# Two layers and an expert block on one core: shared first modulation, rows turned by transposes, modulation pieces moved, constants multiplied in waits

## The reference

```python
for layer in range(2):
    shift_m, scale_m, gate_m, shift_f, scale_f, gate_f = split(silu(c) @ ada_w[layer] + ada_b[layer], 6)
    h = rmsnorm(x, pre_m) * (1 + scale_m) + shift_m
    x = x + gate_m * rmsnorm(mixer[layer](h), post_m)
    h = rmsnorm(x, pre_f) * (1 + scale_f) + shift_f
    x = x + gate_f * rmsnorm((silu(h @ w_gate) * (h @ w_up)) @ w_down, post_f)
# mixer 0: state space model and latent attention; mixer 1: gated linear attention
# (chunks of 64) and sparse attention of three branches (compressed, selected, window)
h = rmsnorm(x); x = x + merged(moba(h), gmlp(h)) @ w_out         # second block
h = rmsnorm(x); m = rmsnorm(mem); x = x + cross_attention(h, m)
h = rmsnorm(x); x = x + peer_ffn(h)                              # 16384 experts, dense here
return rmsnorm(x)
```

## Time and profile before

| | |
|---|---|
| median of 3 runs | 2046.96 us (2045.36 to 2047.48) |
| profiled execution, its own time | 2044.72 us |
| its span | 2042.9 us |
| mean granted TensorE clock | 0.978 of full |
| PE busy | 1922.0 us (94%) |
| DVE busy | 1378.7 us (67%) |
| ACT busy | 986.7 us (48%) |
| POOL busy | 263.4 us (13%) |

### The profile page before, as it was taken

One profiled execution on the slowest core, in us unless ns is written; L12 is line 12 of the kernel. 1 busy time (PEld: TensorE's weight loads), 2 busy tenths in 40 slices (PEclk: granted clock), 3 DMA queues, 4 the chain that ended last, 5 costly groups with the idle time before them and its releaser, 6 DMA issues.

```text
span 2042.9 us, 33499 instructions
## 1 busy us (share of the span) xinstructions
PE 1922.0 (94%) x13340; PEld 1773.0 (87%) x13340; DVE 1378.7 (67%) x2511; ACT 986.7 (48%) x1432; POOL 263.4 (13%) x121
## 2 busy tenths in 40 slices
PE   5899899988998789999998999999999999999998
PEld 5887799988967589998997889999998888999997
DVE  4898765647956664335756548988878887666665
ACT  5445544454435354445554545566653334444444
POOL 1001044430001024441000047100000000000000
PEclk8999999999999799999999999999999999999999
DMA  7663466645654245555444344477776866555452
GB/s 300 228 203 127 157 250 247 234 179 199 205 181 169 73 166 195 186 186 181 165 145 142 127 145 166 166 209 220 219 220 227 300 255 227 187 225 196 176 204 106
DMA packets 94234, 392.82 MB, mean 192 GB/s; under 512 B 7648, under 2 KB 41584, under 8 KB 55552
## 3 DMA queue, kind: packets, MB, share of 16 engines
q1 hardware_dynamic: 94080, 390.69, 55.0%
HBM read 372.83 MB, written 15.73 MB: 190 GB/s over the span
## 4 chain that ended last, share of the span: by engine, by line
PE 75%; DVE 14%; ACT 3%; issue 2%; DMA 0%; POOL 0%; DVEq 0%; ACTq 0%
PE ps L563 10%; PE ps L565 10%; PE ps L564 10%; PE acc L559 9%; PE acc L560 9%; PE acc L561 9%; DVE wlo L1281 3%; PE acc L563 3%; PE acc L565 3%; PE acc L564 3%; DVE arena L1310 2%; PE ps L1236 1%; PE acc L1236 1%; PE ps L626 1%; PE ps L1009 1%
## 5 line engine op out<-in xcount | busy, mean ns | idle before, releaser
L2300 ACT ACTIVATE whi<-raw 128x1024 fp32r<-128x1024 f32 x559 | 589.5, 1059 | 494.3 <-PE acc L561 274.1
L1281 DVE TENSOR_TENSOR wlo<-raw,whi 128x1024 fp32r<-128x1024 f32 x460 | 567.9, 1242 | 312.3 <-ACT whi L2300 311.4
L563 PE MATMUL ps<-hhi,whi 128*128 128x256 f32 x1824 | 521.2, 286 | 9.5 <-ACT hhi L2412 5.4
L564 PE MATMUL ps<-hlo,whi 128*128 128x256 f32 x1824 | 516.6, 283 | 0.0
L565 PE MATMUL ps<-hhi,wlo 128*128 128x256 f32 x1824 | 516.6, 283 | 0.0
L563 PEld LDWEIGHTS ps<-hhi,whi 128*128 128x128 f32 x1824 | 350.2, 192 | 14.6 <-ACT hhi L2412 6.1
L564 PEld LDWEIGHTS ps<-hlo,whi 128*128 128x128 f32 x1824 | 350.3, 192 | 2.9
L565 PEld LDWEIGHTS ps<-hhi,wlo 128*128 128x128 f32 x1824 | 350.1, 192 | 0.0
L1281 POOL TENSOR_TENSOR wlo<-raw,whi 128x1024 fp32r<-128x1024 f32 x99 | 245.2, 2480 | 683.1 <-ACT whi L2300 682.8
L559 PE MATMUL acc<-whi,chi 128*128 128x512 f32 x752 | 295.6, 393 | 3.5 <-DVE wlo L1281 1.9
L560 PE MATMUL acc<-whi,clo 128*128 128x512 f32 x752 | 294.0, 391 | 0.0
(11 more groups left out here) (443 smaller groups left out, 2418.6 us busy)
## 6 DMA issues: line engine op xcount, KB each, us to landing
raw<-in_peer_down SPq DMA_DIRECT2D x64, 1024.0 KB, 5.0
raw<-in_peer_up SPq DMA_DIRECT2D x64, 1024.0 KB, 5.1
arena<-in_ada SPq DMA_DIRECT2D x80, 512.0 KB, 4.8
raw<-in_w_gate SPq DMA_DIRECT2D x22, 1024.0 KB, 4.8
raw<-in_w_up SPq DMA_DIRECT2D x22, 1024.0 KB, 5.2
raw<-in_w_down SPq DMA_DIRECT2D x22, 1024.0 KB, 4.8
arena<-spill SPq DMA_DIRECT2D x14, 1024.0 KB, 7.0
spill<-hT_t SPq DMA_DIRECT2D x22, 448.0 KB, 6.4
```

Source lines behind the costliest of these rows:

```text
L563: e.matmul(out, hi, xh, start=start, stop=False, skip_group_check=True)
L564: e.matmul(out, hi, xl, start=False, stop=False, skip_group_check=True)
L1281: e.tensor_tensor(out=lo, in0=w, in1=hi.bitcast(F32), op=ALU.subtract).then_inc(*X(("lo", j)))
L2300: e.activation(hi, w, ACT.Copy, scale=1.0).then_inc(*self.A(("hi", j)))
```

## The change

1. **First modulation shared.** In every one of the four groups DVE now makes k = 0, 1, 4, 5 and ACT scales k = 2, 3, 6, 7 (`BY_PE`); PE sums ACT's four tiles and DVE's one. DVE adds each group's bias inside the loop of the next one. The slab of `w_low` is loaded before the last 1 MB of the modulation, the first ring piece after the second slab, and the first blocks of `w_low` are cut by DVE instead of POOL.
2. **Rows turned.** `ve_unit` writes x times the root ([128 x 512], two for each half of the tokens) instead of a diagonal, and `pe_norm` turns it with transposes. `pe_rows` uses transposes too.
3. **Order at the junctions.** The block after the first is rounded inside the junction (`se_junction`, `se_norm`), the one after it behind the norm; DVE cuts it after its first pair of tiles.
4. **Modulation's pieces.** The six pieces that hung on `w_nks`, `w_nvs` and `w_out1a` and the one forced before the gate's rows stand in linear attention now, as 2, 3 and 2. In the sparse attention DVE normalises the linear attention's output before it cuts `w_out1a`, cuts a block while ACT exponentiates, and `pct` is turned after the first branch.
5. **Constants in the waits.** Where a junction precedes ffn0, mix1, ffn1, mix2 and the expert layer, PE multiplies a matrix of ones by the constants 16 times before the first half's transposes, 4 times before the second's and 10 times before the first linear layer (`KEEP`).

```diff
+KEEP = (16, 4, 10)
-FIRST = (("w_low", 0, 0), ("w_low", 0, 1), ("w_low", 1, 0), ("w_glr", 0, 0), ("w_mqk", 0, 0))
+FIRST = (("w_glr", 0, 0), ("w_mqk", 0, 0))
+BY_PE = (2, 3, 6, 7)
...
+    def pe_keep(self, e, ps, n):
+        for _ in range(n):
+            e.matmul(ps, self.m.ones, self.m.kc_t[:, 0:128], start=True, stop=True, skip_group_check=True)
...
-    def pe_norm(self, e, nm, x):
+    def pe_norm(self, e, nm, keep=KEEP):
...
         for tt in range(2):
-            e.wait_ge(*self.at("diag", nm, tt))
+            self.pe_keep(e, self.banks.tile(nm, "turned", 3)[:, 128:256], keep[tt])
             for j in range(8):
+                if j % 4 == 0:
+                    e.wait_ge(*self.at("unit", nm, tt, j // 4))
                 o = (j % 2) * 256 + tt * 128
-                i = e.matmul(self.banks.tile(nm, "turned", j // 2)[:, o:o + 128], x[:, tt, j * 128:(j + 1) * 128],
-                             m.diag[:, tt, :], start=True, stop=True, skip_group_check=True)
+                i = e.transpose(self.banks.tile(nm, "turned", j // 2)[:, o:o + 128], m.upd[:, tt, j * 128:(j + 1) * 128],
+                                m.ident)
...
-    def ve_diag(self, e, nm, tt):
+    def ve_unit(self, e, nm, tt, x):
...
+        for half in range(2):
+            sl = slice(512 * half, 512 * half + 512)
+            e.tensor_scalar(out=m.upd[:, tt, sl], in0=x[:, tt, sl], scalar1=m.small[:, 50 + tt:51 + tt], scalar2=None,
+                            op0=ALU.mult).then_inc(*self.V(("unit", nm, tt, half)))
...
         t.then_inc(*self.P(("full", "w_ngate"), ("whole", "w_ngate", 0), ("gated", "P")))
+        self.pe_pieces(e, 2)
...
         self.pe_cmp_hidden(e, 1)
+        self.pe_pieces(e, 3)
         self.pe_cmp_turn(e, 1)
         e.wait_ge(*self.at("out", "gla_state", 2, 2))
         for h in range(4):
+            if h == 3:
+                self.pe_pieces(e, 2)
...
     def se_junction(self, e, post, norm, first):
...
         self.se_acc_square(e, post, 1, 0)
+        self.cut_hi(e, self.W.last(first, 0) + 1)
         self.se_x_square(e, norm, post, 0, 0)
...
         for g in range(4):
             for h in range(2):
+                if (g, h) == (3, 1):
+                    e.dma_start(self.W.slab(0)[0], D["w_low"][0]).then_inc(self.W.slots[0], 16)
```

More of the change, by code:

```diff
@@ L693, in pe_ada, with pe_pieces @@
             i.then_inc(*self.P(("full", "ada", layer, g)))
+    def pe_pieces(self, e, n):
+        for _ in range(n):
+            self.pe_ada(e)
     def pe_ada_until(self, e, layer, part):
@@ L1384, in ve_normed @@
         whole(1)
+        if first:
+            self.cut_lo(e, V, self.W.last(first, 0) + 1)
         low(0)
@@ L1453, in ve_sum @@
         self.ve_eps(e, norm, 0, 48)
-        self.ve_diag(e, norm, 0)
+        self.ve_unit(e, norm, 0, self.m.x)
         self.ve_add_x(e, post, 1, 1)
@@ L1510, in ve_pro @@
             self.ve_eps(e, "mix0", tt, 48)
-            self.ve_diag(e, "mix0", tt)
+            self.ve_unit(e, "mix0", tt, m.x)
         e.wait_ge(self.landed["pos"], 16)
@@ L1874, in ve_nsa @@
                     *V(*([("hvx",)] if ht and j == 3 else [])))
-        self.ve_linear(e, "w_nks", 0, 8, 2)
-        self.ve_linear_tok(e, "w_nvs", 0, 8)
-        e.wait_ge(*self.at("full", "vb"))
-        e.tensor_tensor(out=m.vb, in0=bc(self.banks.tile("vb")[:, 0:64].unsqueeze(1), [128, 8, 64]),
-                        in1=bc(m.kc("ind").unsqueeze(2), [128, 8, 64]), op=ALU.mult).then_inc(*V(("out", "vb")))
+        self.ve_linear(e, "w_nks", 0, 8, 2, ada=False)
         e.wait_ge(*self.at("rstd", "gla"))
@@ L1888, in ve_nsa @@
                 *V(("normed", "gla", j)))
+        self.ve_linear_tok(e, "w_nvs", 0, 8, ada=False)
+        e.wait_ge(*self.at("full", "vb"))
+        e.tensor_tensor(out=m.vb, in0=bc(self.banks.tile("vb")[:, 0:64].unsqueeze(1), [128, 8, 64]),
+                        in1=bc(m.kc("ind").unsqueeze(2), [128, 8, 64]), op=ALU.mult).then_inc(*V(("out", "vb")))
         for eng in "PA":
@@ L1925, in ve_nsa @@
                 self.ve_scores(e, f"nsa{qt}{br}", 8, nk, 0.125, lambda hs, n: m.ab[:, qt, hs, 0:nk], m.St1,
-                               gate=m.ng[:, qt, 8 + 8 * br:16 + 8 * br])
-                self.ve_out(e, "w_out1a", range(at, at + 2))
+                               gate=m.ng[:, qt, 8 + 8 * br:16 + 8 * br],
+                               ahead=self.W.last("w_out1a", 2 * at + 1, 512) + 2)
+                self.ve_out_by_rows(e, "w_out1a", range(at, at + 2), ada=False)
                 self.ve_turn(e, f"nsa{qt}{br}", 8, nk, m.PT1[br])
-            e.wait_ge(*self.at("full", "pct", qt))
-            e.tensor_copy(m.pct, self.banks.tile("pct", qt)[:, 0:128]).then_inc(*V(("out", "pct", qt)))
+                if br == 0:
+                    e.wait_ge(*self.at("full", "pct", qt))
+                    e.tensor_copy(m.pct, self.banks.tile("pct", qt)[:, 0:128]).then_inc(*V(("out", "pct", qt)))
             self.ve_bank_split(e, f"nsa{qt}", m.hH, m.hL, qt)
@@ L2378, in se_junction, with se_norm @@
         self.se_root(e, norm, 1, 48)
-    def se_norm(self, e, nm, src, at=48, ahead=None):
+    def se_norm(self, e, nm, src, at=48, ahead=None, first=None):
         for tt in range(2):
             for half in range(2):
+                if tt and half and first:
+                    self.cut_hi(e, self.W.last(first, 0) + 1)
                 self.se_x_square(e, nm, src, tt, half, at)
@@ L2398, in se_normed @@
         m, A = self.m, self.A
-        if first:
-            self.cut_hi(e, self.W.last(first, 0) + 2)
         for jj in range(4):
@@ L2599, in se_ffn @@
         self.cut_hi(e, self.W.last(f"w_down{layer}", 16 * 11 - 1) + 1)
-        self.se_junction(e, f"ffn{layer}_post", ("mix1", "mix2")[layer])
+        self.se_junction(e, f"ffn{layer}_post", ("mix1", "mix2")[layer], ("w_glr", "w_mqk")[layer])
     def se_mix1(self, e):
@@ L2782, in se_xa @@
         self.se_out(e, "xa_o", range(4), 1)
-        self.se_norm(e, "peer", "xa_o")
+        self.se_norm(e, "peer", "xa_o", first="peer_q")
         A.mark("end", "xa", "A")
```

163 lines of the change are left out of this document (94 added, 69 removed).

## The result

The changed kernel takes 2034.95 us (median of five runs, 2029.4 to 2040.4), the kernel before 2046.96 (2045.05 to 2047.74) beside it: a ratio of 0.9944, with a 95% interval of 0.9923 to 0.9964. It is about 12 us faster, and its runs scatter more. The profiled execution has a span of 2033.1 us against 2042.9, so the traces have 9.8 us of difference to explain.

The account below looks back on a forecast made before the run. It took PE's own instructions, three quarters of the span, as the bound. Terms -3.0 - 4.0 + 2.9 - 2.6 - 3.0 - 5.8 = -15.5 gave 2029.2 us profiled, 2031.5 median; range 2022 to 2043.

Parts of the forecast that it names:

- a stall in linear attention: Linear attention: PE waits for piece 71 ahead of the last head, +6.3, then half clock, +1.7; forecast case, chance 0.48.
- Prologue: First norm: shared modulation brings the coefficients 5.2 us earlier; -3.0 taken, bounds -5.2 and 0.
- two deductions: Prologue: sums starting at half clock (two microseconds), and DVE cutting POOL's blocks (one 1.2 us) ahead of a DVE-bound stretch.
- The four junctions: ffn0, mix1, ffn1, mix2: transposes, early rounding and hidden constants give -1.0 each, -4.0; bounds +1 and -8.
- Expert layer: Expert layer's junction: no wait to fill, 8.8 us of constants and transposes where 5.87 were; +2.9, bounds +2 and +4.
- Rows by transposes: Both feed-forward networks and the very end: transposes take 0.95 us for 1.95; 3 x -0.85 = -2.6, bounds -3 and 0.
- Turning `mem` and `x`: Cross attention: turning takes 1.9 us for 3.73, and the second's bank is free 1.2 earlier; -3.0, bounds -3.3 and 0.
- Pieces: Linear and sparse attention: moved pieces and new order, +3.5 - 7.3 - 2.0 = -5.8; bounds -13.7 and +2.
- no stall: Rival, linear attention: DVE's 12.15 us of idleness hold five pieces if loads keep up; -8, 2023.5, chance 0.20.
- Overlaps absorb: Rival: the DVE-bound stretch swallows the prologue's gain, rounding and cuts the four junctions'; -8.5, 2038.5, chance 0.17.
- Transposes let the clock fall: Rival: each of five first linear layers begins at 1.2 GHz, 2.8 us each, 14 in all; 2045.5, chance 0.07.
- The loads of pieces: Rival, linear attention: three successive loads at 12 us each instead of 4.8, 21.6 more; 2053, chance 0.08.

Follow-up runs that it names:

- e10: Changed kernel with the prologue of before, its loads and their order; only mix0's turning by transposes stays: 2042.8 us, 0.9997 of the kernel before.
- e1: Changed kernel with none of the constants, at the four junctions or the expert layer: 2031.75 us, 0.9938 of the kernel before.
- e2: Changed kernel without constants at the expert layer's junction alone: 2033.49 us, 0.9946 of the kernel before.
- e5: Changed kernel with diagonals back at the five junctions, no constants, early rounding kept: 2033.58 us, 0.9949 of the kernel before.
- e6: Changed kernel without constants, junction transposes replaced by multiplications by the identity, also for `mem` and `x`: 2037.9 us, 0.9974 of the kernel before.
- e11: Changed kernel: last two pieces behind the sums, rounding behind the squares, expert layer's junction as before, 14 constants for 16: 2021.81 us, 0.9896 of the kernel before.
- e4: Changed kernel with modulation pieces back where they were; the new order in sparse attention stays: 2034.45 us, 0.9948 of the kernel before.
- e7: Changed kernel with PE taking linear attention's last two pieces behind the sums of the squares: 2026.92 us, 0.9915 of the kernel before.
- e8: Changed kernel with e5 and e7 together, and DVE waiting for the cos2 and sin2 tables later: 2028.14 us, 0.9926 of the kernel before.

## Why the prediction was right, and where its steps were off

The forecast, 2031.5 from a sum of -15.5, was the case that came: a stall in linear attention, and gains elsewhere that stay. The median shows -12.0, the profiled execution -9.8. Of its signs, PEclk of 1.00 through the four junctions, the 3.8 us at the expert layer and the wait of 5.61 for the piece came; the coefficients came at 36.6, ahead of the 37 to 39. The number is in part luck: the prologue gave more than was put down, and that made good for most of what the four junctions didn't give. The terms:

*Prologue, -3.0: the mechanism right, the size off; measured -5.8, and -6.3 at the first gate's rows.* I had taken two deductions that didn't come. PE doesn't start the sums at half clock, since it has ACT's records right behind the transposes. And no absorption shows in the stretch where DVE is the bound: from the coefficients to the first gate's rows are 183.9 us before and 183.4 after, and e10 gives all of it back. An absorption of a us or two can't be ruled out, since that distance is 182.0 to 187.0 us in the eleven profiles with the new prologue.

*The four junctions, -4.0: the step that failed.* Measured +0.4, -1.9, +0.5, +0.6, so -0.4 in all (mix2 without the wait for the tables: -1.2). The hi block at ffn0 does come 0.9 us earlier after the mixer's end (7.8 to 6.9 us), as forecast. But I wrote that the ten constants "end ahead of ACT's and DVE's first tiles", hidden. They stand behind `banks.take`, which waits for ACT's release, so they end at 245.25, and the first layer starts 11.1 us after the mixer, where it was 10.7 before. Without constants (e1) it starts 0.98 us after DVE's first `hlo` begins (244.25); that instruction begins at 243.04 in the changed kernel, so by estimate some 1.2 us of the ten are in the open at ffn0. At mix2 the first layer does start 1.2 us earlier, as forecast. Nor was there half clock to win in the first layer: before, it took 12.35 us to its 96th record, as after; the 0.50 of the earlier trace rows ended with the turning. The constants mend mostly what comes without them behind the transposes (e1: 13.9 us). At mix1 the gain is real, 0.9 us of an earlier first layer and 1.0 behind it.

*Expert layer, +2.9: measured +3.8.* The reason, constants where there is no wait, is only one of two: without them the clock falls, and 2.7 (e1) to 3.5 (e2) remain. Multiplications on PE, by the diagonal or the identity, keep the clock at this junction and make it short (18.9 and 19.2 in e5 and e6, 18.1 in e11, which is also without the early rounding).

*Rows by transposes, -2.6: right, measured -2.8.* The 8 records take 1.03 us for 1.95, and from the start of the rows to the end of PE's work ahead of the next junction are 6.5 us for 7.4 in the first layer and 6.6 for 7.5 in the second. From the last rows to the end are 11.8 for 12.7.

*Turning `mem` and `x`, -3.0: mostly not there.* From the heads of the third mixer to the turning ahead of the expert layer are 156.2 us before and 155.8 in e11, where that junction is the same: -0.4 for -3.0 (the best profile, e1, has 153.8). From the turning of `mem` to the end of `xa_o` alone are 81.4 us before and 80.5 after, -0.9. Why the rest doesn't show is open.

*Pieces, -5.8: the stall right, the gain behind it too large.* The stall and the half clock were put at 6.3 + 1.7 = 8.0; the stage is 8.0 us longer, with a wait of 5.61. The new order, the pieces out of the sparse attention and the gate's rows were put at -4.5, -7.3 and -2.0, 13.8 in all. Measured are -10.4 up to the start of the gate's rows, of which e4 shows -6.3 for the order and -4.1 for the pieces (in a stage that scatters by 6, see below), and -1.8 from there to the end of the mixer. So the sum is -4.2, not -5.8.

The rivals: "no stall" was wrong for the kernel as changed, and e7 is near what it described, 0.9915 of the kernel before. "Overlaps absorb" had the right number for the junctions, though not by absorption, and was wrong for the prologue. "Transposes let the clock fall" happens without the constants, for 1.5 us at ffn0 and ffn1 and 1.6 (e1) to 2.7 (e2) at peer, not 2.8 each, and with them the clock stays. The loads of pieces did take longer (a median of 5.2 us over all 80, has 4.8), but far from the point from which they decide.

Left open: the scatter. The same code of linear attention took 148.6 to 152.8 us in seven profiles whose pieces were alike, and compressed and sparse attention 68.1 (e7) to 74.1 us (after) with one and the same code there. The latter goes with the clock: from 651.4 to 659.4 us the changed kernel has 0.62, e7 from 648.4 to 656.4 has 1.00. Over the whole stage the granted clock stands at 0.50 for 10.2 us in e5 (the stage takes 69.4) and 13.7 in e7 (68.1), against 17.1 in e8 (71.0) and 20.5 or 23.9 in the eight others (72.9 to 74.1). Why it falls more often in some wasn't tried.

## What to carry to other kernels

A piece of background work put into a wait must be placed behind everything that the critical chain still needs from that engine: with the same two pieces the stage was 8 us longer than without any (140.5) when they stood ahead of the last head, 8 ahead of the sums, and 2.2 to 4.0 (e8, e7, e11) behind them. Work put into a wait to hold the clock paid here only where the wait was long enough for it, and part of that was lost where what it waited for itself (here a bank) pushed it to the end of the wait. Before replacing a multiplication by a cheaper transpose, look at the granted clock of what follows.

## What the runs showed of the hardware

Behind equal waits of TensorE the same records take different times. In the sparse attention 8 records took 1.94 us behind a wait of 3.33 us in the changed kernel, and 1.07 behind 3.34 in e11:
```profile
648.25 1.94 PE L732 MATMUL ps<-kc_t,arena 128*128 128x128 f32 x8 [3.33 <-DVE arena L1521]
```
```profile
642.86 1.07 PE L740 MATMUL ps<-kc_t,arena 128*128 128x128 f32 x8 [3.34 <-DVE arena L1532]
```
So the length of a wait alone, at 3.3 us, doesn't say at which level (1.2 or 2.4 GHz) the records right behind it run. In e11 the clock fell too, but later: it is 0.50 from 645 to 651 us, though PE was busy all that time. Behind the waits of 5.57 to 8.68 us between other work it was 1.2 GHz in all thirteen traces.
